# Low-rank steps of the RWKV projections one unit later, their weights requested ahead of the modulation's pieces

## The chip, the cores and the metric

The kernel runs on one core of a Trainium2 chip. The metric is device time in microseconds (us) of one execution, the median of three runs. A core has five engines that run their own instruction streams and meet at semaphores: TensorE (PE) does matmuls, VectorE (DVE) and ScalarE (ACT) work on tiles, GpSimd (POOL) takes some of that work in later stages, and SyncE (SP) issues the transfers between HBM and on-chip memory. Each engine works through its stream in order: an instruction that waits holds up all behind it.

## The reference

The model is two layers of a transformer-like block over 512 latent tokens and 256 context tokens of width 1024. Only the start of the first layer matters here: the projections of the RWKV-7 mixer.

```
mod_lat = einsum(silu(c), mod_w) + mod_b            # and the same for the context
a = rms_norm(h, g) * (1 + scale) + shift            # 768 tokens, width 1024
xx = centred_shift(a)
xr, xw, xk, xv, xa = (a + xx * mu[i] for i in range(5))
r, k, v = xr @ wr, xk @ wk, xv @ wv                 # three 1024x1024 projections
tanh(xw @ w1[e]); xa @ a1[e]; sigmoid((a + xx * mu[5]) @ g1)    # low rank, 128 columns each
```

The modulation of both layers is a 1024 by 12288 product with two vectors, 48 MB of weights; most of it is read while the projections run.

## The kernel before

The function `rwkv_inputs` computes the projections in 24 units: unit n makes output tile i = n % 8 (128 channels by 768 tokens, with one pad column) of projection m = n // 8 (r, k, v). Each unit sums over eight input tiles k. Every operand is split into a high and a low part, so that one product is three matmul passes (hi*hi, hi*lo, lo*hi), and each tile k takes six matmuls (two halves of the tokens): 48 in a unit.

Three kinds of side work ride in the units:

- The low-rank products, one per phase m, with weights `rw_w1`, `rw_a1`, `rw_g1`. Each is eight steps, step 8m + k for input tile k, and a step is six matmuls that add into banks 4 and 5. `low_steps(n)` lists which steps belong to unit n and behind which tile k of the unit PE does each. A step needs work on three engines first: DVE mixes the input (L749 into `mix_full`, buffer `full[1]`), ACT rounds the weights (L834 `low_rank_hi`) and the mixed input (L837 `low_mix_hi`), DVE subtracts for the low parts (L766 `low_rank_lo`, L770 `low_mix_lo`). There is one buffer for the mixed input, so these of a step begin to write it only when PE is done with the step before. After the last step of a phase, `finish_low(m)` on ACT (L850) applies tanh, copy or sigmoid and frees the banks.
- The mixed input of the next projection, one tile a unit while m < 2: DVE `mix_large`, ACT `round_large` (L827), DVE `rest_large` (L759).
- The modulation: 38 blocks, each of two 512 KB pieces (`mod_raw`, L170) in two buffers, 16 matmuls (L187). `mods_of(n)` puts them behind fixed tiles k, about every fifth one. The pieces of the next block can be requested only when the product of the block before has freed the buffers.

The weights of the projections come in 256 KB halves ("parts"), two a unit, through three buffers (`proj_raw`, L642): ACT rounds a part (L821), DVE subtracts (L733). At the end of a unit ACT and DVE copy the result out of PSUM (L877, L806), and SP stores it (L678). The order on SP is, for unit n: two parts, then the modulation pieces of unit n + 1, then at i = 7 of the first two phases the low-rank weights of the next phase (`load_low`, L648 and L650), then the store of unit n, which waits for its copies. `load_low` waits until DVE has subtracted the last weights of the phase before (`low_rest`), since there is one buffer for all eight tiles. Unit 23 has, before its store, three transfers for the next stage into `full[0]` and `full[1]`. The block of units ends with a barrier of all engines; the next stage (the recurrence) begins with matmuls at L1720.

Of the kernel before, what the change touches and what calls it, by code (L numbers as in the profile page):

```python
# [27 lines left out]
CT = D // P  # L28
# [53 lines left out]
def signal(eng, ins, sem, value):  # L82

    ins.then_inc(sem, 1)
    eng.wait_ge(sem, value)


def need(eng, sem, n):

    if not isinstance(n, int) or n > 0:  # L90
        eng.wait_ge(sem, n)
# [16 lines left out]
class Core:  # L108
# [8 lines left out]
    def sem(self, name):  # L117
        return self.ctx.enter_context(self.nc.semaphore(name))
# [446 lines left out]
def rwkv_inputs(c, d, a, xx, hidden, full, dram, mods_before):  # L565
# [6 lines left out]
    with ExitStack() as ctx:  # L572
        sb = lambda n, s, dt=F32: ctx.enter_context(nc.sbuf_tensor(n, s, dt))
        sem = lambda n: ctx.enter_context(nc.semaphore(n))
        UNITS = 3 * CT
# [16 lines left out]
        shifted, mixed, mix_rounded, mix_rest = (sem(n) for n in ("shifted", "mixed", "mix_rounded", "mix_rest"))  # L592
        low_loaded, low_rounded, low_rest, low_mix_rest, low_product = (sem(n) for n in (
            "low_loaded", "low_rounded", "low_rest", "low_mix_rest", "low_product"))
# [7 lines left out]
        MU_LARGE, MU_LOW = (0, 2, 3), (1, 4, 5)  # L602
        LOW_LOADS = (2, 4, 5)

        def out(n):

            return even_out[:] if n % 2 == 0 else hidden[:, 2, :] if n < UNITS - 1 else xx[:, 0, 0:TOK]

        def low_steps(n):

            m, i = n // CT, n % CT
            tiles = ({0: (), CT - 2: (CT - 3, CT - 2), CT - 1: (CT - 1,)}.get(i, (i - 1,)) if m == 0 else (i,) if m == 1 else
                     {CT - 2: (CT - 2, CT - 1), CT - 1: ()}.get(i, (i,)))
            return [(CT * m + k, (3, CT - 1)[-len(tiles):][at]) for at, k in enumerate(tiles)]

        def mods_of(n):

            count, steps = MOD_BLOCKS - MOD_EARLY, CT * (UNITS - 1)
            places = [(2 * b + 1) * steps // (2 * count) for b in range(count)]
            return [(MOD_EARLY + b, at % CT) for b, at in enumerate(places) if at // CT == n]  # L620
# [5 lines left out]
        def mixed_low(n, nth):  # L626

            return CT + min(n + 1, 2 * CT) + sum(len(low_steps(u)) for u in range(n)) + nth
# [5 lines left out]
        with nc.Block() as block:  # L634
            @block.sync
            def _(sp):
                def load(part):
                    if part < 2 * UNITS:
                        need(sp, w_rest, w_at + part - 2 if part > 2 else 0)
                        n, k = part // 2, HALF_K * (part % 2)  # L640
                        tile = n % CT
                        sp.dma_start(w_raw[part % 3][:], large[n // CT][:, k:k + HALF_K, tile * P:tile * P + P])                            .then_inc(w_loaded[part % 3], 16)  # L642

                def load_low(m):
                    need(sp, low_rest, CT * m)
                    if m < 2:
                        for e in range(2):
                            sp.dma_start(low_raw[:, :, 64 * e:64 * e + 64], small[m][:, :, e, :]).then_inc(low_loaded, 16)  # L648
                    else:
                        sp.dma_start(low_raw[:], small[m]).then_inc(low_loaded, 16)  # L650

                def load_mods(n):
                    for b, _ in mods_of(n) if n < UNITS else []:
                        for i in range(MOD_PARTS):
                            mods.load(sp, b, i)

                load(0)
                load(1)
                load(2)
                load_low(0)  # L660
                load_mods(0)
                for n in range(UNITS):
                    m, i = n // CT, n % CT
                    load(2 * n + 3)
                    load(2 * n + 4)
                    load_mods(n + 1)
                    if i == CT - 1 and m < 2:
                        load_low(m + 1)
                    if n == UNITS - 1:
                        sp.wait_ge(low_product, UNITS)  # L670
                        sp.wait_ge(kept, 16 * 2 * CT)
                        sp.dma_start(full[0][:, 0:TOK], dram[1][:, 0, :]).then_inc(c.first_loaded, 16)
                        for e, low in enumerate(("rw_w2", "rw_a2")):
                            sp.dma_start(full[1][:, e * P:(e + 1) * P], d[low][0].rearrange("e r n -> (e r) n")[:, 0:P])\
                                .then_inc(c.first_loaded, 16)
                    sp.wait_ge(evac_lat, n + 1)
                    sp.wait_ge(evac_ctx, n + 1)
                    sp.dma_start(dram[m][:, i, :], out(n)).then_inc(kept, 16)  # L678
                sp.wait_ge(kept, 16 * UNITS)
# [46 lines left out]
            def _(dve):  # L726
# [3 lines left out]
                def subtract(part):  # L730
                    if part < 2 * UNITS:
                        dve.wait_ge(w_rounded, w_at + part + 1)
                        signal(dve, v.tensor_tensor(w_lo[part % 3][:], w_raw[part % 3][:], w_hi[part % 3][:].bitcast(F32),  # L733
                                                    ALU.subtract), w_rest, w_at + part + 1)
# [13 lines left out]
                def mix(out_, mu, k, done):  # L748
                    signal(dve, v.scalar_tensor_tensor(out_, xx[:, k, :], c.par[:, PMU + 8 * mu + k:PMU + 8 * mu + k + 1],  # L749
                                                       a[:, k, 1:PAD + 1], ALU.mult, ALU.add), mixed, done)  # L750

                def mix_large(q, k):
                    mix(full[0][:], MU_LARGE[q], k, mixed_large(q, k) + 1)
# [32 lines left out]
                for n in range(UNITS):  # L786
                    m, i = n // CT, n % CT
                    subtract(2 * n + 2)
                    if n < CT:
                        shift(i)  # L790
                    if m < 2:
                        mix_large(m + 1, i)
                    for nth, (step, _) in enumerate(low_steps(n)):
                        mix(full[1][:], MU_LOW[m], step % CT, mixed_low(n, nth) + 1)
                        if m < 2 and nth == 0:
                            rest_large(m + 1, i)
                        rest_low(n, nth, step)
                    if m < 2 and not low_steps(n):
                        rest_large(m + 1, i)
                    for b, _ in mods_of(n):  # L800
                        if mods.opens(b) and b > MOD_EARLY:
                            mods.store(dve, mods.batch_of(b) - 1)
                    subtract(2 * n + 3)
                    dve.wait_ge(w_product, w_at + 2 * n + 2)
                    need(dve, kept, 16 * (n - 1))
                    signal(dve, v.tensor_copy(out(n)[:, HALF_TOK:TOK], c.bank[2 * (n % 2) + 1][:, 0:HALF_TOK]), evac_lat, n + 1)  # L806
# [9 lines left out]
            def _(act):  # L816
# [27 lines left out]
                def finish_low(m):  # L844
                    act.wait_ge(low_product, CT * (m + 1))
                    if m == 2:
                        act.wait_ge(kept, 16 * (UNITS - 2))
                    f = (ACT.Tanh, ACT.Copy, ACT.Sigmoid)[m]
                    for b, src, dst, width in PAD_PIECES:
                        nc.scalar.activation(hidden[:, m, dst:dst + width], c.bank[4 + b][:, src:src + width], f)\  # L850
                            .then_inc(small_copied, 1)
# [11 lines left out]
                for n in range(UNITS):  # L863
                    m, i = n // CT, n % CT
                    round_weights(2 * n + 2)
                    if m < 2:
                        round_large(m + 1, i)
                    for nth, (step, _) in enumerate(low_steps(n)):
                        round_low(n, nth, step)
                    for b, _ in mods_of(n):  # L870
                        if mods.closes(b):
                            mods.copy(act, mods.batch_of(b))
                    round_weights(2 * n + 3)
                    act.wait_ge(w_product, w_at + 2 * n + 2)
                    need(act, kept, 16 * (n - 1))
                    for b, src, dst, width in PAD_PIECES[0:2]:
                        ins = nc.scalar.copy(out(n)[:, dst:dst + width], c.bank[2 * (n % 2)][:, src:src + width])  # L877
                    signal(act, ins, evac_ctx, n + 1)
                    if i == (CT - 1 if m < 2 else CT - 2):
                        finish_low(m)  # L880


GROUP = 4
# [2598 lines left out]
```

## Time and profile before

| what | value |
|---|---|
| median of 3 runs (lowest to highest) | 2203.97 us (2200.7 to 2204.55) |
| the profiled execution, its span | 2200.6 us, 2198.8 us |
| PE busy over the span | 2024.7 us (92%) |
| DVE, ACT, POOL busy | 55%, 38%, 17% |
| first to last unit of the projections | 60.68 to 360.85 us of the span |
| PE busy in that stretch | 286.18 of 300.17 us |
| matmuls of the low-rank steps in it | 48 pairs of three passes, 6.0 us of idle time before them |

In a row of a timeline the first number is the start, the second the length, both in us, then engine, line, operation, result<-operands, the shape, and in brackets the idle time of the engine just before and what ended it. A matmul's end is modelled, so matmuls overlap in the rows: the distance from start to start is what one costs.

### The profile page before, as it was taken

To read this page: it belongs to the slowest core of one execution; us is meant where nothing else is said; L and a number is where in the kernel's file an instruction comes from. 1 tells how busy PE (TensorE), PEld (TensorE's weight loads), DVE (VectorE), ACT (ScalarE), POOL (GpSimd) and SP (SyncE) were. 2 spreads that over 40 slices of the span, in tenths; PEclk is the share of its full clock that TensorE was granted. 3 is DMA by queue.
4 is the path that set the end of the run, shared out by engine and by line. 5 is a ranking of instruction groups with operands and counts; after the bars stand their busy time and mean duration, and the time that the engine had idled before them with its cause. 6 is when DMAs were issued, how large, how long until landed. Compare 5 with 4: busy or idle time off the path is not lost. (4 is left out here: it accounts for less than half of the span.)

```text
span 2198.8 us, 52635 instructions
## 1 busy us (share of the span) xinstructions
PE 2024.7 (92%) x22455; PEld 1757.2 (80%) x22455; DVE 1209.7 (55%) x1909; ACT 830.8 (38%) x1395; POOL 366.9 (17%) x387
## 2 busy tenths in 40 slices
PE   5899998799999988699999999998979998999998
PEld 3688886688788887699999999998645577888887
DVE  4864435566666664328767566665576524333333
ACT  2433223455555543226324233234325524422321
POOL 0000000566666662010000000003210010000000
PEclk8899998799999999799999999998989998999999
DMA  9577675001111000421222221212100013332332
GB/s 317 176 226 216 216 233 170 22 19 35 35 35 35 18 11 11 176 62 39 78 77 73 62 77 60 75 58 59 58 29 1 1 58 96 95 111 80 96 113 78
DMA packets 223496, 191.70 MB, mean 87 GB/s; under 512 B 12970, under 2 KB 208180, under 8 KB 222772
## 3 DMA queue, kind: packets, MB, share of 16 engines
q1 hardware_dynamic: 223284, 188.58, 27.5%
q8 instruction: 169, 2.77, 0.5%
q14 instruction: 43, 0.35, 0.1%
HBM read 170.73 MB, written 17.83 MB: 86 GB/s over the span
## 5 line engine op out<-in xcount | busy, mean ns | idle before, releaser
L541 DVE TENSOR_TENSOR ffn_lo<-ffn_raw,ffn_hi 128x1024 fp32r<-128x1024 f32 (+1 forms) x58 | 77.5, 1336 | 196.5 <-ACT ffn_hi L536 196.5
L561 PE MATMUL banks<-operand_hi,ffn_w_hi 128*128 128x384 f32 x464 | 155.7, 336 | 4.4 <-DVE operand_lo L507 4.4
L561 PE MATMUL banks<-operand_lo,ffn_w_hi 128*128 128x384 f32 x464 | 155.6, 335 | 0.0
L561 PE MATMUL banks<-operand_hi,ffn_w_lo 128*128 128x384 f32 x464 | 155.5, 335 | 0.0
L561 PE MATMUL banks<-mix_hi,proj_hi 128*128 128x386 f32 (+1 forms) x384 | 137.1, 357 | 15.5 <-DVE proj_lo L733 10.5
L561 PE MATMUL banks<-operand_hi,ffn_hi 128*128 128x512 f32 x352 | 138.6, 394 | 5.2 <-DVE operand_lo L507 2.8
L561 PE MATMUL banks<-operand_lo,ffn_hi 128*128 128x512 f32 x352 | 138.2, 393 | 0.0
L561 PE MATMUL banks<-operand_hi,ffn_lo 128*128 128x512 f32 x352 | 138.1, 392 | 0.0
L536 ACT CAST ffn_hi<-ffn_raw 128x1024 fp32r<-128x1024 f32 (+1 forms) x60 | 68.4, 1140 | 183.3 <-PE banks L561 182.3
L561 PE MATMUL banks<-mix_hi,proj_lo 128*128 128x386 f32 (+1 forms) x384 | 132.4, 345 | 0.0
L561 PE MATMUL banks<-mix_lo,proj_hi 128*128 128x386 f32 (+1 forms) x384 | 132.2, 344 | 0.0
L431 POOL TENSOR_TENSOR norm_squares<-norm_squares,norm_x 128x768 f32<-128x768 f32 (+1 forms) x18 | 29.8, 1657 | 589.5 <-ACT norm_x L425 589.5
L2827 ACT CAST ffn_w_hi<-ffn_raw 128x512 fp32r<-128x512 f32 (+1 forms) x116 | 68.7, 605 | 130.0 <-PE banks L561 129.9
L2060 POOL TENSOR_TENSOR lvl<-sc_b,level_mask 128x256 f32<-128x256 f32 x144 | 109.9, 779 | 47.5 <-DVE sc_b L1792 33.7
L561 PE MATMUL banks<-ffn_t_hi,ffn_w_hi 128*128 128x384 f32 x320 | 106.9, 334 | 0.0
L561 PE MATMUL banks<-ffn_t_lo,ffn_w_hi 128*128 128x384 f32 x320 | 106.9, 334 | 0.0
L561 PE MATMUL banks<-ffn_t_hi,ffn_w_lo 128*128 128x384 f32 x320 | 106.9, 334 | 0.0
L2994 DVE SCALAR_TENSOR_TENSOR residual_stream<-banks,mod,residual_stream 128x256 f32<-128x256 f32 x144 | 60.8, 478 | 73.3 <-PE banks L561 73.1
L561 PEld LDWEIGHTS banks<-mix_hi,proj_hi 128*128 128x128 f32 x384 | 74.4, 194 | 30.5 <-issue 14.9
L2898 DVE TENSOR_TENSOR ffn_w_lo<-ffn_raw,ffn_w_hi 128x512 fp32r<-128x512 f32 (+1 forms) x112 | 77.5, 694 | 26.6 <-ACT ffn_w_hi L2827 25.0
L561 PEld LDWEIGHTS banks<-operand_hi,ffn_w_hi 128*128 128x128 f32 x464 | 87.7, 189 | 4.7 <-DVE operand_lo L507 4.7
L1808 DVE TENSOR_TENSOR inverse<-banks,inverse 128x256 f32<-128x256 f32 x120 | 50.8, 423 | 73.5 <-PE banks L1578 72.4
(320 smaller groups left out, 5720.9 us busy)
## 6 DMA issues: line engine op xcount, KB each, us to landing
mod_raw<-in_mod_w SPq DMA_DIRECT2D x96, 512.0 KB, 5.2
ffn_raw<-in_ff_w SPq DMA_DIRECT2D x32, 1024.0 KB, 5.3
ffn_raw<-in_ff_w SPq DMA_DIRECT2D x46, 512.0 KB, 3.8
ffn_raw<-in_ff_w SPq DMA_DIRECT2D x16, 704.0 KB, 4.7
proj_raw<-in_rw_wr SPq DMA_DIRECT2D x16, 256.0 KB, 5.8
proj_raw<-in_rw_wk SPq DMA_DIRECT2D x16, 256.0 KB, 6.0
proj_raw<-in_rw_wv SPq DMA_DIRECT2D x16, 256.0 KB, 6.1
rwkv_out_raw<-in_rw_wo SPq DMA_DIRECT2D x8, 512.0 KB, 4.5
```

Source lines behind the costliest of these rows:

```text
L431: pool.tensor_tensor(self.pool_sum[:, self.at0:], self.pool_sum[:, self.at0:], self.x[:, s, self.at0:], ALU.add)\
L536: signal(act, self.nc.scalar.copy(self.hi[s][:, 0:k_tiles, :], self.raw[s][:, 0:k_tiles, :]), self.rounded, self.at + n + 1)
L541: signal(eng, eng.tensor_tensor(self.lo[s][:, 0:k_tiles, :], self.raw[s][:, 0:k_tiles, :], self.hi[s][:, 0:k_tiles, :].bitcast(F32), ALU.s ...
L561: mm = pe.matmul(out, a, b, start=(first and n == 0), stop=(last and n == 2), skip_group_check=onto)
L1808: v.tensor_tensor(x, by_way(work(self.use, "y", G.g, n), n), x, ALU.add).then_inc(x_added, 1)
L2060: g.tensor_tensor(flat(lvl[G.parity][n % 2][:]).rearrange("p (a b x) -> p a b x", **blocks), lower_blocks(sc_b[G.third][:], n), flat(level ...
L2827: nc.scalar.copy(w_hi[x.n % SLOTS][:, 0:x.k_tiles, :], source(x)).then_inc(rounded, 1)
L2898: v.tensor_tensor(w_lo[x.n % SLOTS][:, k, :], source(x), w_hi[x.n % SLOTS][:, k, :].bitcast(F32), ALU.subtract)\
L2994: v.scalar_tensor_tensor(h[:, m, at:at + width], c.bank[bank_no(self, "down", part, m, q)][:, col:col + width], c.mod[:, 0, 40 + m, r:r + ...
```

## The change

`low_steps` now puts step n - 1 into unit n, behind its last tile k = 7, for units 1 to 21; unit 22 has steps 21 (behind k = 3) and 22 (behind k = 7), and unit 23 has step 23 (behind k = 3). Before, in phase 0, unit 6 had steps 5 and 6, and unit 7 step 7; in phase 1 unit n had step n; in phase 2 also, with steps 22 and 23 both in unit 22. The eight steps of a phase now end in the first unit of the next phase, and `finish_low` follows there, for the last phase at the end of unit 23. The low-rank weights of phase m are requested in the phase's first unit instead of the unit before, behind the two weight parts of that unit and ahead of the modulation's pieces. SP's wait ahead of the three early transfers changes with the step that uses `full[1]` last.

```
         def low_steps(n):
-            m, i = n // CT, n % CT
-            tiles = ({0: (), CT - 2: (CT - 3, CT - 2), CT - 1: (CT - 1,)}.get(i, (i - 1,)) if m == 0 else (i,) if m == 1 else
-                     {CT - 2: (CT - 2, CT - 1), CT - 1: ()}.get(i, (i,)))
-            return [(CT * m + k, (3, CT - 1)[-len(tiles):][at]) for at, k in enumerate(tiles)]
+            if n < UNITS - 2:
+                return [(n - 1, CT - 1)] if n else []
+            return [(UNITS - 3, 3), (UNITS - 2, CT - 1)] if n == UNITS - 2 else [(UNITS - 1, 3)]
...
                     load(2 * n + 3)
                     load(2 * n + 4)
+                    if m and i == 0:
+                        load_low(m)
                     load_mods(n + 1)
-                    if i == CT - 1 and m < 2:
-                        load_low(m + 1)
                     if n == UNITS - 1:
-                        sp.wait_ge(low_product, UNITS)
+                        sp.wait_ge(mix_rest, UNITS)
+                        sp.wait_ge(low_mix_rest, UNITS)
...
-                        mix(full[1][:], MU_LOW[m], step % CT, mixed_low(n, nth) + 1)
+                        mix(full[1][:], MU_LOW[step // CT], step % CT, mixed_low(n, nth) + 1)
...
-                    if i == (CT - 1 if m < 2 else CT - 2):
-                        finish_low(m)
+                    if n in (CT, 2 * CT, UNITS - 1):
+                        finish_low(n // CT - (1 if i == 0 else 0))
```

PE's stream in unit 6, behind tile k = 3 (the first two rows are the end of that tile, the last two the start of the next); rows with a minus stood there before:

```order
 L561 MATMUL banks<-mix_lo,proj_hi 128x384
 L561 MATMUL banks<-mix_hi,proj_lo 128x384
-L561 MATMUL banks<-low_mix_hi,low_rank_hi 128x386
-L561 MATMUL banks<-low_mix_lo,low_rank_hi 128x386
-L561 MATMUL banks<-low_mix_hi,low_rank_lo 128x386
-L561 MATMUL banks<-low_mix_hi,low_rank_hi 128x384
-L561 MATMUL banks<-low_mix_lo,low_rank_hi 128x384
-L561 MATMUL banks<-low_mix_hi,low_rank_lo 128x384
 L561 MATMUL banks<-mix_hi,proj_hi 128x386
 L561 MATMUL banks<-mix_lo,proj_hi 128x386
```

PE's stream differs in one other place only, where the same six rows now stand behind tile k = 3 of unit 23; everywhere else the rows are the same, but from unit 6 on the step in them is one earlier by number.

SP's stream around the end of phase 0 before, from the parts of unit 7 to the pieces asked for in unit 8 (`in_rw_a` are the low-rank weights of phase 1):

```order
L642 DMA proj_raw<-in_rw_wk 128x4x128 [waits weights_rest] x2
L170 DMA mod_raw<-in_mod_w 128x4x256 [waits mod_product] x4
L648 DMA low_rank_raw<-in_rw_a 128x8x64 [waits low_rest]
L648 DMA low_rank_raw<-in_rw_a 128x8x64
L678 DMA r_all<-hidden 128x768 [waits proj_ctx_copied,proj_lat_copied]
L642 DMA proj_raw<-in_rw_wk 128x4x128 [waits weights_rest] x2
L170 DMA mod_raw<-in_mod_w 128x4x256 [waits mod_product] x4
```

And the same stretch now:

```order
L641 DMA proj_raw<-in_rw_wk 128x4x128 [waits weights_rest] x2
L170 DMA mod_raw<-in_mod_w 128x4x256 [waits mod_product] x4
L678 DMA r_all<-hidden 128x768 [waits proj_ctx_copied,proj_lat_copied]
L641 DMA proj_raw<-in_rw_wk 128x4x128 [waits weights_rest] x2
L647 DMA low_rank_raw<-in_rw_a 128x8x64 [waits low_rest]
L647 DMA low_rank_raw<-in_rw_a 128x8x64
L170 DMA mod_raw<-in_mod_w 128x4x256 [waits mod_product] x4
```

The low-rank weights moved behind the store of unit 7 and the parts of unit 8; the step that reads them moved from unit 8 to unit 9.

ACT's stream from the copies of unit 22 to the branch that ends the block, before:

```order
L877 COPY proj_out<-banks 128x256
L877 COPY proj_out<-banks 128x128
L850 ACT_TABLE_LOAD
L850 ACTIVATE hidden<-banks 128x256
L850 ACTIVATE hidden<-banks 128x128
L850 ACTIVATE hidden<-banks 128x384
L877 COPY shifted<-banks 128x256
L877 COPY shifted<-banks 128x128
L634 UNCONDITIONAL_BRANCH
```

And now:

```order
L877 COPY proj_out<-banks 128x256
L877 COPY proj_out<-banks 128x128
L834 CAST low_rank_hi<-low_rank_raw 128x128
L837 CAST low_mix_hi<-mix_full 128x769
L877 COPY shifted<-banks 128x256
L877 COPY shifted<-banks 128x128
L850 ACT_TABLE_LOAD
L850 ACTIVATE hidden<-banks 128x256
L850 ACTIVATE hidden<-banks 128x128
L850 ACTIVATE hidden<-banks 128x384
L633 UNCONDITIONAL_BRANCH
```

The table load and the three activations moved behind the copies of the last unit, to the end of the block.

## Rows read from the trace of the kernel before

**Rows 1.** Windows: length, busy time by engine, clock; the stage, units 7, 8
```profile
core 0: us, PE busy (x) PEld busy (x) DVE busy (x) ACT busy (x) POOL busy (x), PEclk, DMA share, GB/s
...
60.68:360.85 300.17, 286.18 (x1916) 249.52 (x1916) 156.76 (x202) 97.58 (x184) 0.00 (x0) 0.97 0.66 206
...
156.21:166.93 10.72, 10.72 (x71) 9.88 (x71) 6.46 (x8) 3.41 (x7) 0.00 (x0) 1.00 0.85 276
166.93:182.46 15.53, 12.84 (x91) 10.90 (x91) 6.33 (x9) 6.47 (x12) 0.00 (x0) 0.99 0.80 227
```

**Rows 2.** Groups of PE's instructions by line in the stage, with idle time before
```profile
L187 PE MATMUL banks<-mod_raw,cond 128*32 128x256 f32 x608 | 42.5, 391 | 3.0 <-DMA mod_raw<-in_mod_w 2.8
L561 PE MATMUL banks<-low_mix_hi,low_rank_hi 128*128 128x386 f32 (+1 forms) x48 | 16.9, 353 | 6.0 <-issue 3.9 <-DVE low_mix_lo L770 2.1
```

**Rows 3.** Timeline of PE at the late steps, units 6, 8, 9 and 16
```profile
148.58 0.41 PE L561 MATMUL banks<-low_mix_hi,low_rank_hi 128*128 128x386 f32 x1 [2.14 <-DVE low_mix_lo L770]
...
181.12 0.42 PE L561 MATMUL banks<-low_mix_hi,low_rank_hi 128*128 128x386 f32 x1 [2.69 <-issue]
181.37 0.34 PE L561 MATMUL banks<-low_mix_lo,low_rank_hi 128*128 128x386 f32 x1
181.55 0.34 PE L561 MATMUL banks<-low_mix_hi,low_rank_lo 128*128 128x386 f32 x1
...
182.46 0.52 PE L561 MATMUL banks<-mix_hi,proj_hi 128*128 128x386 f32 x1
182.78 0.53 PE L561 MATMUL banks<-mix_lo,proj_hi 128*128 128x386 f32 x1
...
279.11 0.42 PE L561 MATMUL banks<-low_mix_hi,low_rank_hi 128*128 128x386 f32 x1 [1.16 <-issue]
```

**Rows 4.** Windows: the stretch behind the stall of unit 8
```profile
182.00:185.50 3.50, 3.50 (x13) 3.50 (x12) 3.36 (x5) 1.50 (x3) 0.00 (x0) 0.51 0.09 29
```

**Rows 5.** Timeline of SP, ACT and DVE: low-rank weights asked for, rounded, used
```profile
170.82 1.26 SPq L648 DMA_DIRECT2D low_rank_raw<-in_rw_a  x2
...
178.80 0.30 ACT L834 CAST low_rank_hi<-low_rank_raw 128x128 fp32r<-128x128 f32 x1 [6.12 <-DMA low_rank_raw<-in_rw_a]
...
180.05 0.96 DVE L770 TENSOR_TENSOR low_mix_lo<-mix_full,low_mix_hi 128x769 fp32r<-128x769 f32 x1 [0.57 <-ACT low_mix_hi L837]
...
276.79 0.30 ACT L834 CAST low_rank_hi<-low_rank_raw 128x128 fp32r<-128x128 f32 x1 [8.59 <-issue]
```

**Rows 6.** Timeline of DVE in unit 6: step 5, then weights part 15
```profile
147.47 0.96 DVE L770 TENSOR_TENSOR low_mix_lo<-mix_full,low_mix_hi 128x769 fp32r<-128x769 f32 x1
...
153.66 0.69 DVE L733 TENSOR_TENSOR proj_lo<-proj_raw,proj_hi 128x512 fp32r<-128x512 f32 x1 [1.78 <-ACT proj_hi L821]
```

**Rows 7.** DMA issues from 169.5, 170.8 and 176.5 us: count, KB, us to landing
```profile
mod_raw<-in_mod_w SPq DMA_DIRECT2D x2, 512.0 KB, 4.3
...
low_rank_raw<-in_rw_a SPq DMA_DIRECT2D x2, 256.0 KB, 6.5
...
mod_raw<-in_mod_w SPq DMA_DIRECT2D x2, 512.0 KB, 6.3
```

**Rows 8.** Timeline of DVE in unit 22: the second step's input
```profile
346.56 0.96 DVE L770 TENSOR_TENSOR low_mix_lo<-mix_full,low_mix_hi 128x769 fp32r<-128x769 f32 x1 [2.11 <-ACT low_mix_hi L837]
```

**Rows 9.** Timeline of ACT, SP, PE to the barrier; landing of the last store
```profile
352.09 1.28 ACT L850 ACT_TABLE_LOAD   x1 [0.52 <-issue]
353.39 0.94 ACT L850 ACTIVATE hidden<-banks 128x256 f32<-128x256 f32 x3
...
360.52 0.54 ACT L877 COPY shifted<-banks 128x256 f32<-128x256 f32 x2 [6.20 <-PE banks L561]
361.16 0.33 SPq L678 DMA_DIRECT2D v_all<-shifted  x1
...
363.92 5.49 PE L1720 MATMUL banks<-hidden,mix_full 64*128 64x256 f32 x16 [3.07 <-PEq L634]
...
v_all<-shifted SPq DMA_DIRECT2D x1, 384.0 KB, 2.3
```

## Prediction
> **What bounds the kernel now.** I read the stage first through windows, then PE's groups by line, then PE's timeline, and only then the engines that PE waits for. The stage of the projections takes 300.2 us, of which PE is busy 286.2 [rows 1]: PE sets the pace, and what a change on the other engines is worth is what it takes out of the 14 us in which PE stands. The groups say where it stands: 6.0 us ahead of the first pass of low-rank steps, 3.0 us ahead of the modulation's products, the rest in the first unit [rows 2]. The 6.0 us are three places: 2.14 us in unit 6, 2.69 us in unit 8, 1.16 us in unit 16 [rows 3]. Unit 7, which has no such place, takes 10.72 us and PE is never idle in it; unit 8 takes 15.53 us [rows 1].
>
> Why PE stands there is on the other engines. In unit 6 two steps share a unit, and the first is due behind tile k = 3: DVE begins its last piece at 147.47 and ends at 148.43, PE starts at 148.58 [rows 6, 3]. In unit 8 the weights of the new phase were asked for at 170.82, ACT waited 6.12 us for them and rounded at 178.80, DVE began the last subtraction at 180.05, PE started at 181.12 [rows 5, 3]. The row of PE says "issue", but it began 0.11 us after that subtraction ended at 181.01, so I read it as that chain. Unit 16 repeats it: ACT rounds at 276.79 after 8.59 us of idleness [rows 5].
>
> **The change part by part.** The span from start to start of full-speed passes is 0.18 us (181.37 to 181.55), while a row lasts 0.34, so each idle time hides 0.16 us more of lost time [rows 3].
>
> Unit 6: step 5 moves from behind k = 3 to behind k = 7, and step 6 to unit 7. Its input was ready at 148.43, and four tiles later PE is past 150. The wait goes: 2.14 + 0.16 = 2.3 us. What is late next? Weights part 15, whose subtraction ends at 154.35 [rows 6]. It is needed in the fifth tile of unit 7. That unit began at 156.21 and would begin 2.3 us plus one step (six passes, 1.06 us) earlier, near 152.9, because one step less stands ahead of it; its fifth tile comes 4 x 1.06 us later, near 157.1. So 2.7 us are to spare. The copies of unit 6 on DVE queue behind that subtraction, but PE needs their bank only in unit 8.
>
> Unit 8: step 7 takes the place of step 8, and its weights have been on the chip since the start of the phase. The wait goes: 2.69 + 0.16 = 2.85 us. PE's clock goes with it. The granted clock is 0.99 over unit 8 with its stall [rows 1], but from 182.0 to 185.5, right behind it, 0.51 of 2.4 GHz, that is the 1.2 GHz level [rows 4]; the passes there are 0.32 us apart (182.46 to 182.78) instead of 0.18 [rows 3]. Eleven passes of 0.14 us more are 1.5 us. The stall of 2.14 us left no such stretch (1.00 in unit 7) [rows 1]; without a stall I expect none. Unit 16 likewise: 1.16 + 0.16 = 1.3 us.
>
> The weights themselves: SP now asks for them behind the store of unit 7 and the parts of unit 8, once DVE has subtracted step 7's weights. I estimate unit 8 to begin at 163.5 (3.4 us earlier than 166.93) and that subtraction about 4 us into the unit, so the request comes near 168.9, and 256 KB halves landed 6.5 us after their issue [rows 7]: about 176, the time unit 9 begins. ACT needs them some 5 us later, and PE behind the unit's last tile, near 186. Margin: over 4 us. The instructions queued behind the waiting request on SP are the pieces of unit 9's first modulation block; those wait for the product of unit 8's second block (near 173) anyway, so the request is out 3 us before. With the low-rank weights, a store and two parts in the queue, such pieces landed after 6.3 us, against 4.3 without [rows 7]: near 179.6, and PE comes to them near 180. I take nothing for this and bound it by 0 and 2 us at each of the two boundaries (the difference of the two rows).
>
> The low-rank queue: rows of 256 bytes in `rw_a1`. The 256 KB halves took 6.5 us where 512 KB pieces of the modulation took 4.3 [rows 7]. The Trainium skill ("DMA: Bandwidth & Descriptors", Specifications) asks for transfers of at least 512 bytes for line rate, and by this rule it is a bad thing to put in front of pieces that PE waits for; the trace agrees with it in those two durations, and the sum by it would lose up to the 2 us above at the first boundary.
>
> Units 22 and 23: the pair of steps in unit 22 stays a pair, and step 23 follows behind k = 3 of unit 23. Its chain is that of the present second step of unit 22, where DVE waited 2.11 us for PE and ACT and worked 0.96 us [rows 8]: 3.1 us at most from the end of the step before on PE. Four tiles give 4.2 us. Cost nothing, or at worst 0.5. SP's early transfers wait for that DVE piece now, which I estimate 6 us ahead of the last copies (360.52); they are read at 363.92 [rows 9], some 9 us after they go out.
>
> The end of the block: the last table load and activations come behind the last copies on ACT. Copies end at 361.06; 1.28 + 0.94 us more [rows 9] put ACT's end at 363.3. The store of unit 23 goes out at 361.16 and lands 2.3 us later, at 363.5, and then PE starts at 363.92 [rows 9]. So the store covers it, by 0.2 us; if the cover were missing, the cost would be 2.2 us. I take 0.1.
>
> The Trainium skill ("ScalarE: Activation LUTs", What ACT_TABLE_LOAD costs) gives 2.66 us for a switch of tables, 1.28 of it the load and the rest a drain. By that ACT would end 1.38 us later, at 364.7, and the block 1.2 us later: the sum would lose 1.2 us. Here 1.30 us lie between the load at 352.09 and the activation at 353.39 [rows 9], with no drain between them.
>
> PE's own work is the same: every step is still done once. Sum: 2.3 + 2.85 + 1.5 + 1.3 - 0.1 = 7.9 us less. Against the profiled execution (2200.6 us, its span plus 1.8) this gives 2192.7. That execution is at the low end of the runs; their median is 2203.97, so I predict **2196.1 us**.
>
> **The rivals.** *Another wait takes the place.* PE runs up to 8 us ahead of the transfers it had waited beside. The modulation already stops PE 3.0 us in all [rows 2], and the stage moves 206 GB/s with 0.66 of the DMA engines' time, 276 GB/s and 0.85 in unit 7 [rows 1]. If the pieces take back 2 us at each boundary and the clock falls there once (1.5 us), 7.9 - 5.5 leaves 2.4; half of that taken back leaves 5: 1.5 to 5.5, 2200.5 as its middle. Against it: the distance from one block's product to the next is set by PE's own tiles, and stays.
>
> *The change doesn't do what it says:* the weights of a phase still arrive late in unit 9 and 17. Then only unit 6's 2.3 us are won, 2201.8. They would have to land 10 us later than estimated.
>
> *Slower.* The wait of the request for DVE holds the modulation's pieces behind it. If DVE comes to step 7's weights only at the end of unit 8, as it came after 178.80 before [rows 5], the pieces go out 5 us late and PE stands for some 5 us and then at half clock (1.5 us) at each of two boundaries, and the low-rank step behind, too: about 13 us against the 8 won, and 2.2 at the block's end, so +5 to +7, about 2210. It decides once the request leaves over 4 us later than 173. Against it: what delayed DVE there was the missing weights, which step 7 doesn't lack.
>
> *The table switch costs more than its row* behind the last copies. Ahead of the load at 352.09 ACT stands 0.52 us [rows 9], and the cover is 0.2; between that loss of 0.3 and the 2.2 of no cover at all lies 1.2 us: 6.7 us won, 2197.3.
>
> **How the numbers follow.** Forecast 0.62, another wait 0.19, late weights 0.06, slower 0.06, table switch 0.07. About 0.2%, 4.4 us, is what a measurement of this kernel can tell from no change. Faster by more: the forecast, the table switch and a third of the second case, 0.74. Within: most of the second case and the third, 0.20. Slower: 0.06. The likeliest case alone has 6.5 to 9.5 us (no late pieces, or 1 us of them), 2194.5 to 2197.5; the runs of one kernel spread over 4 us. The range goes from 2191 to 2203, which takes in all but the slower case and the edge of the runs.
>
> **What would show it.** Right: PE's first pass of a low-rank step has under 1 us of idle time in the whole stage, no stretch at half clock behind unit 8, and the L1720 matmuls start near 356 instead of 363.92, with the stages after it as long as before. Wrong: idle time moved to the modulation's products in units 9 and 17 (another wait), ACT waiting for `low_rank_raw` in unit 9, or ACT's activations ending after the last store has landed.

## The result and the profile after

The changed kernel takes 2191.76 us (median of 5 runs, 2188.26 to 2201.96), the kernel before 2200.7 us (median of 5, 2198.46 to 2204.55): ratio 0.9948, 95% interval 0.9929 to 0.9967. Faster, then: by 8.9 us by the medians, by 11.4 us by the ratio (7.3 to 15.6), an interval that holds the 7.9 us of the sum. The profiled execution took 2192.42 us where the sum put 2192.7, but 2196.1, the sum against the earlier median, is 4.3 us above the measurement.

Windows of the kernel after: the stage, units 7 to 9 (less the end of 9), and the stretch that answers to the one at half clock; the columns are as in [rows 1].

```profile
60.84:352.48 291.64, 284.09 (x1916) 248.21 (x1916) 156.80 (x202) 95.35 (x180) 0.00 (x0) 0.97 0.68 212
153.68:164.39 10.71, 10.71 (x71) 9.87 (x71) 8.41 (x11) 5.37 (x12) 0.00 (x0) 1.00 0.87 279
164.39:176.79 12.40, 12.40 (x91) 10.75 (x91) 6.33 (x9) 3.50 (x7) 0.00 (x0) 1.00 0.73 198
176.79:187.88 11.09, 10.64 (x73) 8.76 (x72) 5.04 (x7) 4.70 (x8) 0.00 (x0) 1.00 0.76 230
176.00:179.50 3.50, 3.50 (x22) 3.50 (x21) 0.84 (x2) 2.96 (x7) 0.00 (x0) 1.00 1.15 291
```

Unit 8 has shrunk from 15.53 us [rows 1] to 12.40, all of it busy, and the clock behind it is 1.00 where it was 0.51 [rows 4]. The groups of PE in the stage show the same as a total:

```profile
L187 PE MATMUL banks<-mod_raw,cond 128*32 128x256 f32 x608 | 42.5, 393 | 2.2 <-DMA mod_raw<-in_mod_w 2.2
L561 PE MATMUL banks<-low_mix_hi,low_rank_hi 128*128 128x386 f32 (+1 forms) x48 | 16.7, 348 | 0.0
```

The 6.0 us ahead of the low-rank steps [rows 2] are 0.0, and PE's idle time for the modulation's pieces fell too, from 3.0 to 2.2. Where those 2.2 stand, and the first matmuls behind the block's end, in PE's timeline:

```profile
182.11 0.64 PE L187 MATMUL banks<-mod_raw,cond 128*32 128x256 f32 x8 [0.34 <-DMA mod_raw<-in_mod_w]
188.67 0.64 PE L187 MATMUL banks<-mod_raw,cond 128*32 128x256 f32 x8 [0.91 <-DMA mod_raw<-in_mod_w]
231.69 0.64 PE L187 MATMUL banks<-mod_raw,cond 128*32 128x256 f32 x8 [0.64 <-DMA mod_raw<-in_mod_w]
281.33 0.64 PE L187 MATMUL banks<-mod_raw,cond 128*32 128x256 f32 x8 [0.36 <-DMA mod_raw<-in_mod_w]
355.53 5.49 PE L1720 MATMUL banks<-hidden,mix_full 64*128 64x256 f32 x16 [3.08 <-PEq L633]
```

Unit 9 has two of them (182.11, 188.67) where it had one of 0.36 us (194.56): the place that the prediction had bounded at 0 to 2 us of loss. In unit 13 the kernel before, in contrast, had two waits where the kernel after has one; these two rows were not among those I read ahead:

```profile
237.41 0.64 PE L187 MATMUL banks<-mod_raw,cond 128*32 128x256 f32 x8 [1.03 <-DMA mod_raw<-in_mod_w]
238.86 0.64 PE L187 MATMUL banks<-mod_raw,cond 128*32 128x256 f32 x8 [0.82 <-DMA mod_raw<-in_mod_w]
```

The low-rank weights of phase 1 in the kernel after, on DVE, SP and ACT, and the landings of the requests from 170 and from 174 us (count, KB, us from a request's start):

```profile
168.70 0.29 DVE L766 TENSOR_TENSOR low_rank_lo<-low_rank_raw,low_rank_hi 128x128 fp32r<-128x128 f32 x1
170.01 4.01 SPq L647 DMA_DIRECT2D low_rank_raw<-in_rw_a  x2
174.25 3.05 SPq L170 DMA_DIRECT2D mod_raw<-in_mod_w  x2
182.58 0.30 ACT L834 CAST low_rank_hi<-low_rank_raw 128x128 fp32r<-128x128 f32 x1
...
low_rank_raw<-in_rw_a SPq DMA_DIRECT2D x2, 256.0 KB, 7.6
...
mod_raw<-in_mod_w SPq DMA_DIRECT2D x1, 512.0 KB, 6.4
```

The first half was asked for at 170.01 (I had 168.9), the second at 170.92; they landed after 7.0 and 8.3 us, the second near 179.2 (I had 176). ACT rounds at 182.58, behind another rounding and without a wait, and PE reads the product from 189.25 on. SP was 4.01 us at these two requests, up to 174.02; the first piece behind them left at 174.25, just when PE was done with the first half of the product that frees the buffers (173.55, 1.07 us long in all). They landed after 6.4 us, as the 6.3 of [rows 7] had it, the second piece at 182.06, and PE waited for it (182.11 above). The end of the block:

```profile
352.16 0.54 ACT L877 COPY shifted<-banks 128x256 f32<-128x256 f32 x2 [8.06 <-PE banks L561]
352.72 1.28 ACT L850 ACT_TABLE_LOAD   x1
354.02 0.93 ACT L850 ACTIVATE hidden<-banks 128x256 f32<-128x256 f32 x3
352.78 0.33 SPq L678 DMA_DIRECT2D v_all<-shifted  x1
```

From the last copies to L1720 are 3.37 us (352.16 to 355.53) where there were 3.40 [rows 9].

Unit by unit, as lengths from the unit's first pass to the next unit's, with the start of L1720 (us, from PE's timeline; the kernels are told of below; tail_long is the kernel after up to unit 22, and differs from it only in the end of the block):

| kernel | unit 6 | 8 | 9 | 13 | 16 | 17 | L1720 |
|---|---|---|---|---|---|---|---|
| before | 15.37 | 15.52 | 13.83 | 14.06 | 13.75 | 12.73 | 363.9 |
| before_a | 14.89 | 16.31 | 14.87 | 13.72 | 13.70 | 12.66 | 365.8 |
| before_b | 16.78 | 14.21 | 13.15 | 14.43 | 13.60 | 12.38 | 364.2 |
| before_pad | 15.41 | 14.88 | 12.60 | 12.39 | 13.41 | 12.49 | 363.5 |
| pair | 13.32 | 15.01 | 14.10 | 15.96 | 14.79 | 12.76 | 365.4 |
| order | 14.54 | 12.39 | 12.54 | 15.86 | 12.35 | 12.50 | 360.0 |
| steps | 12.01 | 12.40 | 16.87 | 12.65 | 12.35 | 15.95 | 365.1 |
| after | 11.95 | 12.39 | 13.62 | 12.79 | 12.34 | 12.48 | 355.5 |
| again | 11.93 | 12.40 | 12.95 | 12.88 | 12.35 | 12.54 | 354.8 |
| after_pad | 11.91 | 12.40 | 13.90 | 13.64 | 12.35 | 12.67 | 356.8 |
| tail_long | 11.99 | 12.40 | 12.59 | 13.09 | 12.38 | 13.26 | 359.1 |

Unit 6 of the kernels with moved steps does 1.06 us less work, which unit 23 does instead.

### The profile page after: what moved, and what is told of

It reads as the page before. It is cut to its first block and busy times, and to the rows that moved or that the text cites. A ratio compares the mean times of both kernels' runs of the same rounds, so it can differ in the third digit from the quotient of the medians.

```text
span 2190.7 us, 52634 instructions
## 1 busy us (share of the span) xinstructions
PE 2022.6 (92%) x22455; PEld 1755.4 (80%) x22455; DVE 1209.5 (55%) x1909; ACT 830.5 (38%) x1395; POOL 365.9 (17%) x387
## 3 DMA queue, kind: packets, MB, share of 16 engines
q8 instruction: 169, 2.77, 0.5%
```

## The experiments

Theory: the three waits for low-rank steps go because each step has a unit more, and the phase's weights arrive in time because they stand ahead of the pieces; the rest of the gain comes from the modulation's waits. Rivals were the request order alone, unit 6 alone, or a chance of the runs.

**again** is the kernel after, run once more.

> The changed kernel once more, beside the partial versions on the same chip. Theory (the saving is PE's stalls of units 6, 8 and 16 and nothing after the stage): 8 to 9 us less than the kernel before, ratio 0.9960 to 0.9964 with an interval that holds it, the stage's end (the first L1720 matmul) 8 to 9 us earlier, and the stretch from there to the end as long as before within 1 us. Rival (a part of the saving lies behind the stage, in a higher granted clock): ratio near 0.995, and the stretch behind the stage 2 to 3 us shorter.

2191.66 us (median of 8) against 2201.67 (of 31), ratio 0.9948 (0.993 to 0.9966); L1720 at 354.8, no idle time ahead of a low-rank step. The gain is no chance of one set of runs. The ratio is the one that the rival named, but its reason isn't there: the stretch behind L1720 is 1835.8 us long, not shorter than the 1834.9 before.

**pair** is the kernel before with step 5 of unit 6 two tiles later:

```
-            return [(CT * m + k, (3, CT - 1)[-len(tiles):][at]) ...
+            return [(CT * m + k, (5 if n == CT - 2 else 3, CT - 1)[-len(tiles):][at]) ...
```

> The kernel before, with one number changed: in unit 6 step 5 stands behind tile k = 5 instead of k = 3. Theory: the stall of 2.14 us ahead of it goes and the two others stay: stage end 2.3 us earlier, ratio 0.9990. Rival (the stall is not the place of the step but DVE's load with two steps in one unit): a stall of 1 to 2 us turns up ahead of step 6 behind k = 7 of the same unit, and under 1 us is won.

2200.98 us, ratio 0.9986 (0.9968 to 1.0004). The wait of unit 6 is gone (13.32 us for 15.37), and those of units 8 and 16 stand, the second twice as long:

```profile
179.83 0.42 PE L561 MATMUL banks<-low_mix_hi,low_rank_hi 128*128 128x386 f32 x1 [2.39 <-issue]
...
280.87 0.42 PE L561 MATMUL banks<-low_mix_hi,low_rank_hi 128*128 128x386 f32 x1 [2.21 <-issue]
```

Unit 13 lost 1.9 us more, in part at a lower clock (0.66 from 238.0 to 241.5 us), and L1720 came at 365.4. Unit 6 alone is worth 2 us in its place and nothing at the end that these runs can tell.

**order** is the kernel before with the low-rank weights requested ahead of the pieces, in units 7 and 15:

```
-                    load_mods(n + 1)
                     if i == CT - 1 and m < 2:
                         load_low(m + 1)
+                    load_mods(n + 1)
```

> The kernel before, with the low-rank weights of the next phase asked for ahead of the modulation's pieces in units 7 and 15, and no step moved. Theory: the request goes out near 161 instead of 170.8, ACT no longer waits for it, the stalls of units 8 and 16 shrink from 2.69 and 1.16 to under 0.3 us and the stretch at half clock goes: 5.0 to 5.7 us won, ratio 0.9975; the stall of unit 6 stays. Rival (the steps have to move, since the request waits for DVE and holds the modulation's pieces): under 3 us won, with PE waiting 2 us or more for the pieces of unit 8.

2197.26 us, ratio 0.9978 (0.9962 to 0.9995). Units 8 and 16 have the lengths of the kernel after (12.39, 12.35): the request alone takes these waits away. Unit 6 keeps its wait, and unit 13 has both of its own:

```profile
148.35 0.41 PE L561 MATMUL banks<-low_mix_hi,low_rank_hi 128*128 128x386 f32 x1 [1.29 <-DVE low_mix_lo L770]
...
233.07 0.64 PE L187 MATMUL banks<-mod_raw,cond 128*32 128x256 f32 x8 [1.31 <-DMA mod_raw<-in_mod_w]
234.51 0.93 PE L187 MATMUL banks<-mod_raw,cond 128*32 128x256 f32 x8 [0.80 <-DMA mod_raw<-in_mod_w]
```

That is 0.22% of the 0.52%, with the steps where they were; L1720 comes 4.6 us ahead of the mean of the kernel before (364.6, below). So in units 8 and 16 moving the steps adds nothing to moving the request. What the kernel after has over this one is unit 6 (1.5 us, without the work that moved) and unit 13 (3.1 us, of which the experiment with the packets below tells).

The prediction read the 6.5 us of the low-rank halves [rows 7] as a cost of their rows of 256 bytes. This run shows that the rows alone don't make it: asked for at 160.61 us, ahead of the pieces, the same rows landed after 3.5 and 4.6 us:

```profile
low_rank_raw<-in_rw_a SPq DMA_DIRECT2D x2, 256.0 KB, 4.1
```

**steps** is the kernel after with the request behind the pieces:

```
+                    load_mods(n + 1)
                     if m and i == 0:
                         load_low(m)
-                    load_mods(n + 1)
```

> The changed kernel with the low-rank weights asked for behind the modulation's pieces of units 9 and 17 instead of ahead of them; the steps stay one unit later. Theory: the request then waits for the product of a modulation block in unit 9 and goes out near 183 instead of 170, the weights land near 189, and PE stands 3 to 6 us ahead of the last step of unit 9, the same in unit 17, with half clock behind it: 2 to 5 us of the 8 are left at unit 6, ratio 0.998 to 1.002. Rival (moving the steps alone does it): no stall ahead of a step, ratio as the changed kernel.

2201.46 us, ratio 0.9995 (0.9982 to 1.0009): the whole gain is gone. The waits of units 8 and 16 reappear in units 9 and 17, longer:

```profile
191.82 0.66 PE L561 MATMUL banks<-low_mix_hi,low_rank_hi 128*128 128x386 f32 x1 [3.82 <-issue]
...
289.70 0.41 PE L561 MATMUL banks<-low_mix_hi,low_rank_hi 128*128 128x386 f32 x1 [3.28 <-issue]
```

As expected, the clock fell behind both (0.72 from 192.7 to 196.2 us, 0.56 from 290.6 to 294.1). So the request ahead of the pieces carries more than the unit's delay does: without it the delay only moves the wait. (Two more combinations were not run: the later steps with the request left in unit 7, and order together with pair.) This is the prediction's second rival, and the order on SP is what keeps it from coming true.

**before_a** and **before_b** are the kernel before, profiled again, to see how far one trace stands for it.

> The kernel before, profiled once more. Theory (the first profiled execution was a short one in this stage: the saving is larger in the median because the waits of the stage vary): the first L1720 matmul starts at 365 to 368 us instead of 363.92, with a stretch at half clock behind the double wait for the modulation in unit 13 (as the kernels with unmoved steps showed it), or a wait of 2 us instead of 1.16 in unit 16. Rival (the stage is the same each time and the rest of the saving lies behind it): the matmul starts within 0.7 us of 363.92, and the stretch behind it is 2 to 3 us longer than 1835.

> The same as before_a, a second time, to see the spread of the stage's end: theory 365 to 368 us in at least one of the two, rival both within 0.7 us of 363.92.

2199.18 and 2196.59 us. L1720 at 365.8 and 364.2, a mean of 364.6 over the three traces, against 355.1 for the two of the kernel after: 9.5 us in the stage. The waits differ from trace to trace, 1.51 to 2.14 us in unit 6 and 1.56 to 2.77 in unit 8; in unit 13 all have 1.0 us or more. Here that of before_a:

```profile
240.78 0.64 PE L187 MATMUL banks<-mod_raw,cond 128*32 128x256 f32 x8 [1.58 <-DMA mod_raw<-in_mod_w]
```

The 365.8 of before_a is in the range of the theory, but not for its reasons: the wait of unit 13 has the full clock behind it, unit 16 waits 1.10 us, and the time is in units 8 and 9, with 17 passes at half clock and a wait of 1.03 us for a piece. before_b has full clock behind unit 8, and half clock behind the wait of unit 6 instead:

```profile
149.90:153.40 3.50, 3.50 (x13) 3.50 (x13) 1.75 (x3) 0.83 (x1) 0.00 (x0) 0.54 0.99 332
```

Behind L1720 the spans are 1834.9, 1831.6 and 1830.6 us before and 1835.2 and 1835.8 after. This stretch, which the change doesn't touch, varies by as much as half of the effect, so a single execution can't size it.

**tail_long** is the kernel after with the last three activations on ACT done three times, to measure the cover of the last store:

```
+                    if n == UNITS - 1:
+                        act.wait_ge(small_copied, 9)
+                        for more, (b, src, dst, width) in enumerate(2 * PAD_PIECES):
+                            signal(act, nc.scalar.activation(hidden[:, m, dst:dst + width], ..., ACT.Sigmoid), ...)
```

> The changed kernel with the last three sigmoid activations done three times at the end of the block, the same values each time: about 2 us more on ACT behind the last copies. Theory (the landing of the last store covers ACT's tail by only 0.1 to 0.2 us): the barrier moves by nearly all of the addition, the first L1720 matmul comes 1.6 to 2.0 us later behind the start of the last copies than in the changed kernel (3.4 us). Rival (the cover is longer than the rows say): under 1 us later.

ACT's last rows, the store's landing, and the first matmuls behind the barrier (five lines further down in this kernel):

```profile
353.33 0.54 ACT L877 COPY shifted<-banks 128x256 f32<-128x256 f32 x2 [8.06 <-PE banks L561]
...
356.15 2.46 ACT L884 ACTIVATE hidden<-banks 128x256 f32<-128x256 f32 x6
...
v_all<-shifted SPq DMA_DIRECT2D x1, 384.0 KB, 2.3
...
359.09 3.30 PE L1725 MATMUL banks<-hidden,mix_full 64*128 64x256 f32 x10 [5.47 <-PEq L633]
```

From the copies to the matmuls are 5.76 us against 3.37: 2.39 us more for work that ends 2.49 later (356.12 to 358.61), so the store covered the activations by 0.1 us, and all beyond is paid in full (one run, 2193.76 us). That is above the 1.6 to 2.0 us of the theory, since the work was longer than the 2 us assumed.

**parts** is the kernel after with the pieces cut in half, in four buffers (`MOD_DEEP, MOD_PARTS = 4, 4`).

> The changed kernel with the modulation's blocks in four pieces of 256 KB through four buffers instead of two of 512 KB through two: the same memory, but a piece is asked for once a quarter of the block's product is done. Theory (what is left of PE's waits in the units are these pieces, 2.2 us): the waits fall to under 1 us, 1 to 2 us won over the changed kernel, ratio to the kernel before 0.9940 to 0.9946. Rival (76 more transfers to issue and smaller ones hold SP and the DMA queues up): the waits grow, 1 us or more is lost.

2202.75 us, ratio 1.0006 (0.999 to 1.0022). The weight loads' group (the idle time that ends with a piece's landing) of the kernel after, and then of parts:

```profile
L187 PEld LDWEIGHTS banks<-mod_raw,cond 128*32 128x32 f32 x608 | 15.6, 111 | 20.1 <-issue 10.1 <-DMA mod_raw<-in_mod_w 4.7
```

```profile
L187 PEld LDWEIGHTS banks<-mod_raw,cond 128*32 128x32 f32 x608 | 17.0, 111 | 28.3 <-DMA mod_raw<-in_mod_w 13.9 <-issue 10.1
```

The rival holds: with more and smaller requests the waits got longer, not shorter, and L1720 came at 364.6. Whether their number or their size did it isn't shown.

**after_pad and before_pad** ask why unit 13 got shorter, though the change touches nothing there. In the trace a packet of 16 KB (2.77 MB in 169 packets) comes on a queue of instructions every 256 instructions of PE on average (14 distances in the projections of the kernel before, 205 to 302), so I take it for PE's instructions. In the kernel before one falls beside the pieces of unit 13, in the kernel after behind them, since the change moves 12 instructions out of unit 6. The DMA queues in the half microsecond from 233.8 us before (packets, MB, share of 16 engines), with the landing of the pieces issued at 231.59:

```profile
q8 instruction: 1, 0.02, 22.0%
...
mod_raw<-in_mod_w SPq DMA_DIRECT2D x2, 512.0 KB, 6.3
```

and from 231.0 us after, where the pieces had gone out at 225.70 and 226.13, and landed at 229.24 and 231.65:

```profile
q8 instruction: 1, 0.02, 12.1%
...
mod_raw<-in_mod_w SPq DMA_DIRECT2D x2, 512.0 KB, 4.5
```

The first packet held 22% of 16 engines for 0.5 us, 1.8 us of one engine's time. The two kernels move it by waits that are met already, on PE in unit 6: 24 behind k = 3 in the kernel after (shown), 96 behind k = 2 in the kernel before, where PE stands anyway. In the traces they are 12 and 48 instructions:

```
+                        if n == 6 and k == 3:
+                            for _ in range(24):
+                                pe.wait_ge(mix_rest, 1)
```

> The changed kernel with 24 waits on a semaphore that is long satisfied, on TensorE's queue in unit 6 behind the projection step k=3, which put the later instructions of that queue back about to where they stood in the kernel before, so that TensorE's instruction packet (16 KB on the DMA engines) falls beside the modulation's pieces of unit 13 again. Theory (the packet's collision with the pieces makes the long wait of unit 13): the wait comes back as a double one, at least 1.0 us and then at least 0.6 us, and the pieces there land in about 6.3 us instead of 4.5. Rival (the packet is not the cause): unit 13 keeps a single wait of about 0.6 us. By either, the low-rank steps stay without a wait, and the stage's end lies at 355 to 357 us.

> The kernel before with 96 waits on a semaphore that is long satisfied, on TensorE's queue in unit 6 behind the projection step k=2, where TensorE waits for the low-rank step anyway; the instruction packet of unit 13 then falls ahead of the time at which the modulation's pieces are asked for. Theory (collision): unit 13's wait shrinks to a single one under 0.8 us, and the stage ends 1 to 1.5 us earlier than the kernel before's mean of 364.6 us. Rival (the packet is not the cause): unit 13 keeps 1.0 to 1.4 us and 0.8 us behind it. By either, the waits of the low-rank steps stay (about 2, 2 to 2.7 and 1 us).

after_pad: the packet comes 3.1 us behind the request in unit 13 (225.39), the pieces land after 6.0 us, and the wait is double again, though smaller than I expected (one run, 2198.17 us):

```profile
230.95 0.64 PE L187 MATMUL banks<-mod_raw,cond 128*32 128x256 f32 x8 [0.77 <-DMA mod_raw<-in_mod_w]
232.26 0.64 PE L187 MATMUL banks<-mod_raw,cond 128*32 128x256 f32 x8 [0.67 <-DMA mod_raw<-in_mod_w]
```

before_pad: the packet comes ahead of the request (232.38), the pieces land after 4.3 us, and unit 13 takes 12.39 us (one run, 2193.85 us). L1720 is at 363.5, within what the theory expected. The 48 instructions take the place of the wait in unit 6, which is as long as before (15.41 us). But the packets of units 11 and 19 now fall beside pieces, issued at 209.61 and 304.08, which land after 5.7 and 5.6 us:

```profile
216.97 0.64 PE L187 MATMUL banks<-mod_raw,cond 128*32 128x256 f32 x8 [0.93 <-DMA mod_raw<-in_mod_w]
238.00 0.64 PE L187 MATMUL banks<-mod_raw,cond 128*32 128x256 f32 x8 [0.25 <-DMA mod_raw<-in_mod_w]
311.73 0.64 PE L187 MATMUL banks<-mod_raw,cond 128*32 128x256 f32 x8 [1.22 <-DMA mod_raw<-in_mod_w]
```

Both ways the wait follows the packet: unit 13 takes 13.64 to 15.96 us in the six traces in which a packet comes 2.1 to 3.2 us behind the request of its pieces (the three of before, pair, order, after_pad) and 12.39 to 13.09 in the five without (after, again, tail_long, steps, before_pad). These are single traces; the three of the kernel before differ by 0.7 us there, the three of the kernel after by 0.3. The wait of 1.57 us in unit 9 of after_pad (188.37) has no packet beside it; its cause stays open.

**spaced** is an attempt at a better kernel: the blocks of the modulation exactly five tiles apart instead of four or five.

```
-            count, steps = MOD_BLOCKS - MOD_EARLY, CT * (UNITS - 1)
+            count, steps = MOD_BLOCKS - MOD_EARLY, CT * UNITS - 2
```

> The changed kernel with the modulation's blocks spread so that each stands five tiles behind the one before, where six of the distances were four tiles. Theory (the waits that are left, in units 9, 13 and 16, stand where a block follows the one before after four tiles and its pieces have a tile's time less to land): those waits go, the weight loads' idle time for the pieces falls from 4.7 to about 2 us, the stage ends 1.5 to 2.5 us earlier than 355 us, and the ratio to the kernel before is 0.993 to 0.994. Rival (the waits are set by the landing alone and follow it to the new places): no gain, ratio 0.995 and the weight loads' idle time 4 us or more.

2194.64 us (median of 6) against 2204.37 (of 11), ratio 0.9956 (0.9939 to 0.9973), L1720 at 355.8. The waits went to units 7 and 10:

```profile
163.20 0.64 PE L187 MATMUL banks<-mod_raw,cond 128*32 128x256 f32 x8 [0.77 <-DMA mod_raw<-in_mod_w]
...
200.82 0.64 PE L187 MATMUL banks<-mod_raw,cond 128*32 128x256 f32 x8 [0.85 <-DMA mod_raw<-in_mod_w]
```

The weight loads' idle time for pieces is 4.7 us as before it. My theory on the distances fell: no gain.

## Why the prediction was right in kind and wrong in size

*Unit 6*: 2.3 us predicted for the wait. 15.37 to 11.95 is 3.42, less the 1.06 that moved to unit 23: 2.36. Right; pair shows it alone (2.05).

*Unit 8 and the half clock behind it*: 4.35 predicted, 3.13 in unit 8 and 0.21 in unit 9 measured. The wait and the low clock are gone as said; the waits for pieces in unit 9 (0.34 and 0.91, for one of 0.36) took back 0.9 of the 1.0 us that is missing. The first of them, which again doesn't have, comes of the request ahead of the pieces: SP took 4.01 us for the low-rank weights where it had taken 1.26 [rows 5], so that the pieces had a margin of 0.2 us behind it and not the predicted 3, and they landed 2 us later than in steps (180.68 and 182.06 for 178.81 and 180.22), where they go ahead of it. Why the second got longer isn't shown. That is the loss of 0 to 2 us which I had named and then taken as nothing.

*Unit 16*: 1.3 predicted, 13.75 to 12.34, 1.41 measured.

*The clock*: that a stall of 2.14 us leaves no half clock held in that trace alone; in before_b it stood behind a stall of 2.05 us in unit 6, and not behind the 1.56 us in unit 8. So the 1.5 us is a term that comes and goes between executions of the kernel before.

*The low-rank weights in time*: right, with 3.4 us to spare on ACT (179.2 to 182.58) though they took 8.3 us to land and not 6.5. Why they are slow was read wrongly: the same rows landed after 3.5 and 4.6 us in order, so the two durations of [rows 7] don't show a cost of short rows. steps shows what it costs when they are later.

*The tail*: 0.1 predicted, nothing measured (3.37 for 3.40 us); tail_long shows the cover of 0.1 to 0.2 us that the prediction read from the rows. The load starts 0.02 us behind the copies and the activations 0.02 us behind the load, so the drain by which the Trainium skill ("ScalarE: Activation LUTs", What ACT_TABLE_LOAD costs) would have lost 1.2 us was not there.

*The step that failed* is the modulation's: "I take nothing for this and bound it by 0 and 2 us", a loss at two boundaries and zero elsewhere. Measured, it was 1.0 lost at the first boundary, nothing at the second, and 1.27 won in unit 13, where I hadn't looked; 0.25 more in unit 17 and 0.60 in units 18 to 22 came without a wait of low-rank steps. So the units give 2.36 + 3.34 + 1.27 + 1.41 + 0.25 + 0.60 = 9.2 us against 7.9. In the two profiled executions 0.9 of it is hidden, because that of before was 0.9 us ahead when unit 6 began; L1720 moved by 8.4. Over the three traces of before and two of after it is 9.5. Unit by unit, over three traces each (with tail_long), the change gives 2.7 in unit 6, 3.9 in units 8 and 9, 1.1 in unit 13, 1.3 in unit 16, -0.2 in unit 17 and 0.6 in units 18 to 22. So the loss at the boundaries is nearer 0.5 and 0.2 us, and what the zero missed is above all unit 13, where the packet's place had changed.

*The level* is the second step that failed, and in us the larger one: "their median is 2203.97, so I predict 2196.1". That is the median of three runs; with five it was 2200.7, and 2201.67, 2201.93 and 2204.37 in the later sets. Against the 2200.7 beside it, 2196.1 stands for a gain of 4.6 us, where the medians gave 8.9. Of the miss of 4.3 us, 3.3 is that median (2203.97 - 2200.7) and 1.0 the sum (8.9 - 7.9). The ratio, which this hardly touches, was 0.9964 by the prediction and lies just inside both intervals. Whether the 11.4 us of the ratio are really more than the stage's 9.5 stays open: the interval holds both.

*The rivals*: "another wait" came true for 1.0 us and was outweighed; the slower case didn't come, since DVE took step 7's weights at 168.70 and the request was out by 174.02, 0.2 us ahead of the pieces' turn and not 4 us behind it; the table switch cost nothing.

## What to carry to other kernels

When a step is given more time, look at what its request stands behind in the queue as well: the delay without the reordering (steps) won nothing, the reordering without the delay (order) won less than half. A wait elsewhere that is a race between a transfer and a fixed slot can change when instructions are moved far ahead of it, so read all waits of that kind ahead of the prediction and give the term a sign of either kind. And set a predicted difference against several traces and as many runs as there are: here the median of three runs was 3.3 us off that of five, over a third of the effect.

## What the runs showed of the hardware

Instruction packets of PE compete with data for the DMA engines. In four traces (before, after, before_pad, after_pad, 140 to 345 us) 85 pairs of pieces went out back to back (requests under 0.6 us apart): 21 with a packet from 0.5 us ahead of their request to 4 us behind it, which landed after a median of 5.1 us, and 64 without, after 4.4 us. The Trainium skill ("Runtime: NRT & Kernel Launch", Instruction fetch mechanics) says that an engine's instructions are refilled in 16 KiB blocks of 256, through a queue of its own, at a cost that is mostly hidden. The trace agrees with the size and the distance; hidden it was not for PE's waits for pieces: with the packet's place unit 13 got 0.85 us longer (after to after_pad) and 1.67 us shorter (before to before_pad).

The granted clock behind a stall of PE was not the same in each execution. Behind unit 8 it was 0.51 (stall of 2.69 us, before), 0.50 (2.77, before_a) and 1.00 (1.56, before_b); behind the first stall of unit 6 it was 1.00 (2.14, before) and 0.54 (2.05, before_b). Behind the two waits of unit 13 it was 1.00 in the kernel before (1.03 and 0.82 us) and 0.53 in order (1.31 and 0.80; 234.5 to 238.0 us). What decides between the two levels isn't shown.
